# Softmax probabilities turned by a transposing DMA instead of by TensorE, in a fused block of FFNs and attention mixers

## The reference

```python
# first mixer: 8 heads, only the 64 keys chosen by an index score
s = jnp.einsum('bqhd,bqkhd->bhqk', qb, k_sel).astype(jnp.float32) * att_scale
s = jnp.where(valid[:, None], s, -jnp.inf)
p = jax.nn.softmax(s, axis=-1).astype(v.dtype)
return jnp.einsum('bhqk,bqkhd->bqhd', p, v_sel)
```

## Time and profile before

| what | value |
|---|---|
| median of 3 runs | 1520.27 us (1520.24 to 1520.3) |
| the profiled execution | 1520.18 us |
| its span in the trace | 1518.1 us |
| busy: TensorE, VectorE, ScalarE, GpSimd | 99%, 42%, 31%, 68% |
| granted TensorE clock, mean | 0.999 of full speed |
| weights loaded | 290.83 MB on SP's queue, 54.5% of the DMA engines' time |

### The profile page before, as it was taken

The page is one execution under the profiler, slowest core; times in us unless marked ns, Lnnn a source line. Parts: engine busy times, 40 slices in busy tenths (PEclk is TensorE's granted clock), DMA queues, the critical chain, the costliest instruction groups (busy, mean ns, idle before and its releaser), DMA issues.

```text
span 1518.1 us, 32667 instructions
## 1 busy us (share of the span) xinstructions
PE 1510.1 (99%) x13880; PEld 1174.1 (77%) x13882; DVE 637.6 (42%) x1509; ACT 475.0 (31%) x1243; POOL 1027.0 (68%) x565
## 2 busy tenths in 40 slices
PE   9999999999999999999999999999999999999998
PEld 7666888898666866669889966669888889888885
DVE  4332385445332333315844533325454535464532
ACT  3221163413221132204541232213443313343322
POOL 6976667667767677775586677773858565648653
PEclk9999999999999999999999999999999999999999
DMA  9665554455655565555545465664455554546551
GB/s 390 224 212 200 183 189 173 167 179 217 210 200 198 192 237 207 194 202 196 175 167 186 176 236 194 204 211 156 161 198 193 183 195 155 177 150 239 170 192 56
DMA packets 42625, 293.96 MB, mean 194 GB/s; under 512 B 4720, under 2 KB 5232, under 8 KB 8688
## 3 DMA queue, kind: packets, MB, share of 16 engines
q1 hardware_dynamic: 41760, 290.83, 54.5%
q10 hardware_dynamic: 720, 1.04, 0.2%
HBM read 290.81 MB, written 1.05 MB: 192 GB/s over the span
## 4 chain that ended last, share of the span: by engine, by line
PE 97%; DVE 2%; ACT 1%; issue 0%; DVEq 0%
PE ps L774 26%; PE ps L656 15%; PE ps L657 15%; PE ps L658 15%; PE ps L775 13%; PE ps L675 1%; PE ps L677 1%; PE ps L676 1%; PE ps L869 1%; PE ps L889 1%; ACT ps L1308 1%; PE ps L823 0%; PE ps L734 0%; PE ps L824 0%; PE ps L825 0%; PE ps L851 0%
## 5 line engine op out<-in xcount | busy, mean ns | idle before, releaser
L626 POOL TENSOR_TENSOR w_low<-ring 128x1024 f16<-128x1024 f32 (+1 forms) x544 | 1008.2, 1880 | 379.0 <-DMA ring<-in_w 378.7
L656 PE MATMUL ps<-hP,ring 128*128 128x256 f16 (+1 forms) x1936 | 469.1, 257 | 0.8 <-DVE work L1957 0.4
L657 PE MATMUL ps<-hP,ring 128*128 128x256 f16 (+1 forms) x1936 | 468.9, 257 | 0.0
L658 PE MATMUL ps<-hP,w_low 128*128 128x256 f16 (+1 forms) x1936 | 468.8, 257 | 0.0
L774 PE MATMUL ps<-hP,ring 128*128 128x512 f16 x1280 | 416.3, 380 | 0.0
L775 PE MATMUL ps<-hP,w_low 128*128 128x256 f16 x1280 | 349.2, 273 | 0.0
L774 PEld LDWEIGHTS ps<-hP,ring 128*128 128x128 bf16 x1280 | 125.0, 98 | 151.5 <-issue 0.4
L656 PEld LDWEIGHTS ps<-hP,ring 128*128 128x128 bf16 x1936 | 189.9, 98 | 23.3 <-issue 5.4
L657 PEld LDWEIGHTS ps<-hP,ring 128*128 128x128 bf16 x1936 | 189.2, 98 | 15.6
L658 PEld LDWEIGHTS ps<-hP,w_low 128*128 128x128 f16 x1936 | 189.2, 98 | 15.5
L774 PE MATMUL ps<-work,ring 128*128 128x512 f16 x528 | 171.8, 380 | 0.0
(11 more groups left out here) (277 smaller groups left out, 1740.8 us busy)
## 6 DMA issues: line engine op xcount, KB each, us to landing
ring<-in_w SPq DMA_DIRECT2D x261, 1024.0 KB, 4.8
ring<-in_w SPq DMA_DIRECT2D x12, 512.0 KB, 3.6
con<-in_const SPq DMA_DIRECT2D x1, 2812.0 KB, 18.3
gm<-in_gm SPq DMA_DIRECT2D x2, 1024.0 KB, 17.8
ring<-in_w SPq DMA_DIRECT2D x2, 768.0 KB, 4.9
ring<-in_w SPq DMA_DIRECT2D x2, 560.0 KB, 5.4
ring<-in_w SPq DMA_DIRECT2D x2, 544.0 KB, 3.5
xT<-in_x SPq DMA_DIRECT2D x3, 256.0 KB, 4.1
```

The source lines that it names most:

```text
L626: nc.gpsimd.tensor_tensor(w_low[:, c % SLOTS, a:b], ring[:, c % SLOTS, a:b], w_high[:, c % SLOTS, a:b], ALU.subtract).then_inc(split.by((c ...
L656: nc.tensor.matmul(bank, w_high[:, slot, a:a + m], rhs(k, 0), start=(k == 0), stop=False)
L657: nc.tensor.matmul(bank, w_high[:, slot, a:a + m], rhs(k, 1), start=False, stop=False)
L658: mm = nc.tensor.matmul(bank, w_low[:, slot, a:a + m], rhs(k, 0), start=False, stop=(k == kt - 1))
```

## The change

The probabilities are written by `normalise` as 16-bit high parts (`probsP`, on the place of `probs`), and a new `lows` adds their low parts, both from the exps in PSUM. ScalarE then issues one transposing DMA for the unit, which turns all 24 blocks of 128 x 128 (four heads, high and low, three blocks each) into `probsTP`; `mix` waits for that DMA. `turn` on TensorE, `copy_turned` and `low_turned` are gone. In the second mixers `mix` stands later: "s" behind four "bk" and two "bv" tiles, "w" behind "kcmp", "vcmp" and merge(0,0), "b" behind merge(0,7). The scores of "b" and all that follows stand one or two merges later, on the three engines alike. In ScalarE's order the DMA stands where `copy_turned` stood, except in "w" (behind "hid" 0) and "b" (behind merge(0,4)).

```diff
+        probsP = work[:, 0:4 * PACK].bitcast(F16).rearrange("p (h s n) -> p h s n", h=4, s=2)
+        probs_turned = ctx.enter_context(nc.semaphore("probs_turned"))
-        turned = signal("turned", units)
-        turned_copied = signal("turned_copied", units)
-        turned_low = signal("turned_low", units)
+        in_turn = {unit: i + 1 for i, unit in enumerate(units)}
...
-                def turn(s, u):
-                    pe.wait_ge(*probs_ready.at((s, u)))
-                    for h in range(4):
-                        for a in range(0, PACK, P):
-                            mm = nc.tensor.transpose(ps[:, 4 + h, a:a + P], probs[:, h, a:a + P], const("ident"))
-                    mm.then_inc(turned.by((s, u)), 1)
...
                 def mix(s, u, v_of, high, low):
                     pe.wait_ge(*v_split.at((s, v_of)))
-                    pe.wait_ge(*turned_low.at((s, u)))
+                    pe.wait_ge(probs_turned, 16 * in_turn[s, u])
...
-                    turn(s, "s")
                     gemm("dq", 1), gemm("dk", 0)
-                    mix(s, "s", "cvg", lambda t, h: c_vg_h[:, t, 0:HD], lambda t, h: c_vg_l[:, t, 0:HD])
                     for n in range(4):
                         gemm("bk", n)
                     gemm("bv", 0), gemm("bv", 1)
+                    mix(s, "s", "cvg", lambda t, h: c_vg_h[:, t, 0:HD], lambda t, h: c_vg_l[:, t, 0:HD])
...
-                    turn(s, "w")
                     gemm("hid", 0), gemm("hid", 1), gemm("dg", 1)
-                    mix(s, "w", "cvg", lambda t, h: c_vg_h[:, t, HD:P], lambda t, h: c_vg_l[:, t, HD:P])
                     gemm("kcmp", 0), gemm("vcmp", 0)
                     merge(0, 0)
+                    mix(s, "w", "cvg", lambda t, h: c_vg_h[:, t, HD:P], lambda t, h: c_vg_l[:, t, HD:P])
+                    merge(0, 1)
                     pe.wait_ge(*mixed_taken.at((s, "w")))
                     pe.wait_ge(*taken(s, ("bq", 3)))
                     scores(s, "b", lambda h: b_qT[:, h, :], lambda h: b_kT[:, h, :])
-                    merge(0, 1), merge(0, 2), merge(0, 3)
-                    turn(s, "b")
-                    merge(0, 4), merge(0, 5)
+                    for n in range(2, 8):
+                        merge(0, n)
                     mix(s, "b", "bv", lambda t, h: b_v_h[:, t, h * HD:h * HD + HD],
                         lambda t, h: b_v_l[:, t, h * HD:h * HD + HD])
-                    merge(0, 6)
+                    merge(1, 0)
...
-                def copy_turned(s, u):
-                    act.wait_ge(*turned.at((s, u)))
-                    nc.scalar.activation(probsTP[:, :, 0, :], ps[:, 4:8, 0:PACK], ACT.Copy).then_inc(turned_copied.by((s, u)), 1)
+                def turn(s, u):
+
+                    act.wait_ge(*probs_ready.at((s, u)))
+                    act.dma_start_transpose(probsTP[:, :, :, :].rearrange("p h s (a q) -> p (h s a) q", q=P),
+                                            probsP[:, :, :, :].rearrange("p h s n -> p (h s n)")).then_inc(probs_turned, 16)
...
+                    take("dk", 1)
                     exps(s, "w")
-                    take("dk", 1), take("dv", 0), take("dv", 1)
+                    take("dv", 0), take("dv", 1)
                     gate("dg", 0)
-                    copy_turned(s, "w")
-                    take("hid", 0), take("hid", 1)
+                    take("hid", 0)
+                    turn(s, "w")
+                    take("hid", 1)
                     gate("dg", 1)
                     take("kcmp", 0)
-                    merge(0, 0), merge(0, 1)
+                    merge(0, 0), merge(0, 1), merge(0, 2)
                     exps(s, "b")
-                    merge(0, 2), merge(0, 3)
-                    copy_turned(s, "b")
-                    merge(0, 4), merge(0, 5)
+                    merge(0, 3), merge(0, 4)
+                    turn(s, "b")
+                    merge(0, 5), merge(0, 6), merge(0, 7)
                     y_parts(1)
...
-                        ins = nc.vector.tensor_tensor(probs[:, :, a:b], ps[:, 4:8, a:b], r, ALU.mult)
+                        ins = nc.vector.tensor_tensor(probsP[:, :, 0, a:b], ps[:, 4:8, a:b], r, ALU.mult)
+                    chain.link(ins)
+
+                def lows(s, u):
+                    for h in range(4):
+                        for t, (a, b) in enumerate(HALVES):
+                            ins = nc.vector.scalar_tensor_tensor(probsP[:, h, 1, a:b], ps[:, 4 + h, a:b], sums[:, t, h:h + 1],
+                                                                 probsP[:, h, 0, a:b], ALU.mult, ALU.subtract)
                     ins.then_inc(probs_ready.by((s, u)), 1)
-
-                def low_turned(s, u):
-                    dve.wait_ge(*turned_copied.at((s, u)))
-                    nc.vector.tensor_tensor(probsTP[:, :, 1, :], ps[:, 4:8, 0:PACK], probsTP[:, :, 0, :], ALU.subtract
-                                            ).then_inc(turned_low.by((s, u)), 1)
...
+                    merge(0, 1)
                     dve.wait_ge(*scores_ready.at((s, "b")))
...
                     biggest(s, "b")
-                    merge(0, 1)
+                    merge(0, 2)
                     normalise(s, "b")
-                    merge(0, 2), merge(0, 3)
-                    low_turned(s, "b")
-                    merge(0, 4), merge(0, 5)
+                    lows(s, "b")
+                    for n in range(3, 8):
+                        merge(0, n)
                     dve.wait_ge(*mixed.at((s, "b")))
```

More of the change, by code:

```diff
@@ L1133, in mixer_b @@
                     mm.then_inc(cmp_scores.by(s), 1)
-                    merge(0, 7), merge(1, 0)
+                    merge(1, 1), merge(1, 2)
                     pe.wait_ge(*cmp_probs.at(s))
@@ L1141, in mixer_b @@
                     mm.then_inc(cmp_turned.by(s), 1)
-                    merge(1, 1)
+                    merge(1, 3)
                     pe.wait_ge(*cmp_copied.at(s))
@@ L1148, in mixer_b @@
                     mm.then_inc(cmp_mixed.by(s), 1)
-                    merge(1, 2)
+                    merge(1, 4)
                     pe.wait_ge(*y_low.at((s, "c")))
@@ L1155, in mixer_b @@
                     mm.then_inc(stick_scores.by(s), 1)
-                    for n in range(3, 8):
+                    for n in range(5, 8):
                         merge(1, n)
-                    merge(2, 0)
+                    merge(2, 0), merge(2, 1), merge(2, 2)
                     pe.wait_ge(*stick_low.at(s))
@@ L1169, in mixer_b @@
                     mm.then_inc(stick_sums.by(s), 1)
-                    merge(2, 1), merge(2, 2), merge(2, 3)
+                    merge(2, 3), merge(2, 4), merge(2, 5)
                     pe.wait_ge(*stick_probs.at(s))
                     mix_values(lambda t, h: d_v[:, t, h * HD:h * HD + HD]).then_inc(stick_mixed.by(s), 1)
-                    for p in range(20, 32):
-                        if s == LAST_STAGE and p == 22:
+                    for p in range(22, 32):
+                        if s == LAST_STAGE and p == 23:
                             pe.wait_ge(*y_low.at((s, "d")))
@@ L1529, in mixer_b @@
                                          ACT.Copy).then_inc(cmp_copied.by(s), 1)
-                    merge(1, 1)
+                    merge(1, 3)
                     y_parts(2)
-                    merge(1, 2), merge(1, 3)
+                    merge(1, 4), merge(1, 5)
                     act.wait_ge(*stick_z.at(s))
@@ L1535, in mixer_b @@
                     nc.scalar.activation(ps[:, 4:8, 0:PACK], ps[:, 4:8, 0:PACK], ACT.Ln, bias=1.0).then_inc(stick_ln.by(s), 1)
-                    for p in range(12, 18):
-                        if p == 15:
+                    for p in range(14, 20):
+                        if p == 17:
                             act.wait_ge(*stick_sp.at(s))
@@ L1542, in mixer_b @@
                     nc.scalar.activation(probsT, ps[:, 4:8, 0:PACK], ACT.Exp).then_inc(stick_probs.by(s), 1)
-                    merge(2, 2), merge(2, 3)
+                    merge(2, 4), merge(2, 5)
                     y_parts(3)
-                    for p in range(20, 24):
-                        if s == LAST_STAGE and p == 22:
+                    for p in range(22, 24):
+                        if s == LAST_STAGE and p == 23:
                             for i in range(4):
@@ L1863, in mixer_a @@
                     normalise(s, 0)
-                    low_turned(s, 0)
+                    lows(s, 0)
                     y_parts(0)
@@ L1874, in mixer_a @@
                     normalise(s, 1)
-                    low_turned(s, 1)
+                    lows(s, 1)
                     dve.wait_ge(*deviation.at(s))
@@ L2026, in mixer_b @@
                     low("qc", 1), low("kc", 0)
+                    lows(s, "a")
                     for t in range(TT):
@@ L2040, in mixer_b @@
                     normalise(s, "s", gates_c(1))
+                    lows(s, "s")
                     gate("bg", 1)
@@ L2054, in mixer_b @@
```

(21 more changed lines are left out.)

19 lines of the change are left out of this document (6 added, 13 removed), and 2 rows, old and new, of the table DVE_TAKES.

## The result

The changed kernel takes **1574.99 us** (median of 4 runs, 1573.5 to 1575.7), the kernel before 1520.26 beside it: ratio 1.0359, 95% interval 1.0346 to 1.0371. That is 55 us slower, where 1509 and a range of 1503 to 1549 were forecast. The profiled execution took 1573.5 us, its span 1571.4.

What follows compares the result with a forecast made beforehand. TensorE, busy 99% of the span, was taken to bound the kernel: 1520.2 - 17.2 removed + 2.8 DMA waits + 2.8 VectorE wait = 1508.6, with half a microsecond for contention 1509 us; range 1503 to 1549.

Steps and rivals of the forecast that it cites:

- `lows`: VectorE's new low-part instructions, eight in a unit: 3.3 us per unit, standing between the normalisation and the DMA.
- Removed 17.2 us: TensorE: 144 transposes gone, 15.7 us, plus 1.5 us of waits for the normalised probabilities.
- the DVE wait: Unit "b": TensorE's sixth merge product waits for VectorE's merge(0,3), 1.4 us, 2.8 us over both stages.
- Moves: Step on the reordered products, scores, merges and copies: new order priced at nothing, at most 1 us a stage at merge(0,0).
- The margin priced at nothing: Weights of merge(0,0), split on POOL: margin about 0 after the move, priced 0, at most 1 us per stage.
- The rooms: Time from DMA issue to the product of values in each unit: 4.1 to 6.3 us, 7.7 with unit "b"'s wait.
- X: Transposing DMA's time from issue to landing: taken as 4.9 us for 768 KB, giving back 2.8 us of TensorE waits.
- my upper end of 8.8: Upper end kept for the DMA's landing time, in us, from a 512 KB load that ran among the weights.
- the block rule: Skill's 1.309 us per 128 x 128 block through the DMA crossbar: 31.4 us for 24 blocks, about 1820 us in all.
- Rival 1: Ahead of `mix`: the DMA lands late; slower from 6.5 us landing, 1549 us at 8.8; chance 0.24.
- Rival 2: ScalarE's queue is held while the DMA is issued, so takes behind it are late: 16.2 us, 1525 us; chance 0.12.
- the one at the deviation: First mixers: with ScalarE held, the deviation for the gMLP norm comes 1.5 us too late.

## Why the prediction was wrong

- **Removed 17.2 us, and the DVE wait.** Right in the sum: 1506.5 without the DMA, where 17.2 less the new wait of 2.8 gives 1505.8. But the wait behind `lows` was 0.7 us a stage instead of 1.4, and another 0.7 a stage came ahead of merge(0,0), so that the sum came out right by luck, two errors of opposite sign. The second is a step missing under "Moves": the values' product of "w" (1.1 us), now moved behind merge(0,0), had covered the gate of "dg" 1. The margin priced at nothing for GpSimd at merge(0,0) held: TensorE did not wait for it there.
- **`lows`.** Right: 4 x 0.474 + 4 x 0.343 = 3.3 us.
- **The rooms.** Roughly right, 0.4 to 0.8 us too small: unit 0 of A0 had 8.8 - 3.6 = 5.2 where 4.8 stood, "s" had 1132.1 - 1127.2 = 4.9 (its two waits left out) where 4.1 stood.
- **X, the term that failed.** "I take 4.9, by size": it landed in 9.0, just above my upper end of 8.8. Bytes were the wrong measure. The plain copy of the same bytes took 4.4, and without weights beside it the transposing one, with its 3104 small packets, took 2 to 3 us more than the plain one. The waits ahead of the products of values came to some 28 us in all (the mix gaps less 0.2 each), 25 more than forecast. For the block rule I cited (the Trainium skill, VectorE: DVE Perf Modes, section "The three transpose paths"), which gives one block, I had worked out 31.4 us for 24 of them in a row as an estimate. The trace does not agree with that multiplication: 5.4 to 6.5 us alone, 9.0 beside the weights. (Rival 1's sum has 43.0 in one line and 43.4 in the next; the 0.4 us change nothing.)
- **Rival 2, held to be 0.12 likely, happened beside rival 1.** "No DMA issue of this trace shows as work of ScalarE" was an argument from plain DMAs: in the run with a plain copy it holds its queue 0.47 us, the transposing one 4.1. The hold's price was 10.3 and 10.9 us at "w" and 1.8 at "s" in both stages; I had 3.2 and 2.4. One more of its predicted waits shows, 1.05 us ahead of merge(0,7) in B1 alone; the one at the deviation does not. The size at "w" failed because I set the hold equal to a landing of 4.9 and never asked what SyncE's loads do to it there; the plain copy too took over 10 us to land at "w". The page of the Trainium skill that I named beside it (DMA: Bandwidth & Descriptors, section "Why a DMA increments its semaphore by 16 and not by 1") counts the cost of such a DMA as time of the issuing sequencer. The trace agrees in kind: the issuing queue is held 3.6 and 3.8 us by the 768 KB without company.
- **The clock, not priced at all.** 13.5 us: behind eight of the ten longest waits the products went at 1.2 GHz. The prediction has no term for it; the dummy products gave 8.2 of it back.
- **The range.** Its upper end took rival 1 alone at 8.8 us. The three effects come together: 1506.5 + 28 (landing) + 25 (hold: 21 at "w", 3 at "s", 1 at "b") + 13.5 (clock) is 1573.0, against the profiled 1573.5.

What the chances missed: when a gain is put at risk by one unseen operation, the alternatives are not exclusive: both rivals hang on the same transfer, and a late one is also a long hold.

## What to carry to other kernels

Don't price a transposing DMA by its bytes: here 24 blocks cost 5.4 to 6.5 us alone and 12 blocks 3.6 to 4.2. Charge the hold of its issuing queue to whatever stands behind it; issue it from a queue whose next instruction can wait, and place it ahead of the large loads that it would otherwise run beside. Where TensorE is the bound, add to each expected wait of several microseconds the half-clock stretch that follows. Here the whole DMA from SyncE's queue gained nothing (1521.5 us); cutting it in two by heads, so that the first starts before the second is computed, gave 1514.7, and its place in the queue 1507.9, of a bound of 1506.5.

## What was not expected of the hardware

- A transposing DMA occupies the queue of the engine that issues it: 3.6 to 4.6 us for 768 KB in ten of the twelve issues of the changed kernel, 12.0 and 12.6 in the other two, at "w"; without company 3.6 and 3.8, and 1.3 and 1.4 for 384 KB, less than half. A plain one: 0.5 us, at "w" too.
- The landing differs with the queue that issues it: 9.0 us in the median from ScalarE's, 7.1 from SyncE's, where the weights' next load stands behind it. Whether it is the queue or the loads in flight stays open.
- Versions with SyncE's DMAs scatter more from run to run (1518.98 to 1526.62 and 1512.69 to 1518.56) than the kernel before (1520.03 to 1520.56); the last version less (1507.61 to 1509.27). In the first of these the mean granted clock goes with the time: 0.999 in the three executions of 1518.98 to 1519.13 us, 0.995 in that of 1526.62, so the slower one spent more of its time at half the clock. What sets that off in one execution and not in another stays open.
